# The down product of a decoder layer as seven products of halves, with sums of activations made in gate and up

## The chip, the cores and the metric

The kernel runs on one core of one Trainium2 chip. The metric is the device time of one execution in microseconds (us); less is better. Three runs of the kernel before gave 2863.46, 2863.54 and 2865.74, median 2863.54 us. TensorE is the matmul engine, VectorE (DVE), ScalarE (ACT) and GpSimd (POOL) are the elementwise engines, and SyncE (SP) issues most of the DMAs.

## What is computed

One inference step of a decoder layer over 2048 prompt tokens and 8 sample tokens, all in float32. The part that matters here is its last:

```
def swiglu(h, w_gate, w_up, w_down):
    return (jax.nn.silu(h @ w_gate) * (h @ w_up)) @ w_down

xp = xp + mix_out(y_conv, y_fox, y_mem, out_norm_g[l], w_out[l])
xp = xp + swiglu(rmsnorm(xp, norm2_g[l]), w_gate[l], w_up[l], w_down[l])
y_prompt = rmsnorm(xp, final_norm_g)
```

The width D is 1024 and D_FF is 2816, so `w_gate` and `w_up` are 1024 x 2816 and `w_down` is 2816 x 1024. The projections, the attention and the output product come ahead of it.

## The kernel before

The program runs in stages with a barrier of all engines between them: `project_all`, `attend`, `combine`, `gate_up`, `down`. Each float32 product is three matmuls on split operands: a high part (`_hi`, made by ScalarE) and a rest (`_lo`, made by VectorE or GpSimd): hi x hi, hi x lo, lo x hi.

**gate_up** (from about 1440 to 2340 us). The tokens are cut into three slices of 2 x 344, 2 x 344 and 2 x 340 (`WIDTHS`, `STARTS`); in a slice the two halves a11/a21 and a12/a22 are the two halves of the tokens against two blocks of 128 rows of D_FF. An item is one product of 256 columns of `w_gate` (even g) or `w_up` (odd g) with a slice. 22 items make a slice, 66 the stage. Each item is done by seven products of halves (`ORDER`: b11, t2, t3, t1, b21, t4, b22), 12 matmuls each. The weights of an item (1 MB) come by `weights(g)` on SP into `raw[g % 2]`; GpSimd makes four combinations t1 to t4 (`combos`, L2312 to L2317) and the rest of two base blocks (`base_lo`, L2325); ScalarE makes the high parts (`base_hi` L2357 and L2358, `combos_hi` L2348), VectorE the rests (`combos_lo` L2414, L2424). VectorE adds up the seven products: u2 (L2459), u3 (L2465), u4 (L2474), and the four quarters (L2436). For a gate item the quarters go to `silu`; for an up item each is multiplied at once with its `silu` (L2440), and after the fourth `s.act` is raised. SP waits for that and stores the quarters into `act_turned`, two DMAs of 128 x 2 x 344, and in the last slice two small ones with the 8 sample tokens (L2297).

What sets the order on SP: in iteration g it first issues the weights of item g + 2, then, if g is an up item, waits for `s.act` and issues the stores. So the weights of the gate item g + 3 are issued right behind the stores of the up item g. GpSimd takes up the combinations of g + 2 after those of g + 1 were split (`t_lo`), since there is one buffer for them; ScalarE splits them after its copy of b11 (L2387).

**down** (2341 to 2859 us). The product is done in two halves of 512 columns, each over 16 tiles of 128 tokens: 32 groups (n) of 22 x 3 matmuls of 128 x 512 (L2836 to L2838). The 22 weight blocks of a half stay on chip; the first 8, and the activations of tile 0, are loaded ahead, in gate_up. A tile of activations is 1.4 MB in rows of 512 B. Residual rows come from DRAM (`x1`), the half sum goes back to `x1` and is read again for the second half, where the final norm follows (ScalarE square, GpSimd root, VectorE scaling).

## Time and profile before

| | us |
|---|---|
| median of three runs | 2863.54 |
| span of the profiled execution | 2858.8 |
| gate_up, about | 900 |
| down, first to last matmul | 506.7 (2343.7 to 2850.4) |

| engine | busy us | share |
|---|---|---|
| TensorE | 2690.6 | 94% |
| VectorE | 1712.7 | 60% |
| GpSimd | 1610.4 | 56% |
| ScalarE | 1172.5 | 41% |

The profile is one execution, and its times count from the start of its span. Busy shares are means over stages. A row of a timeline has the start, the duration, the engine, the line and what was written from what was read; a bracket at its end says how long the engine stood idle ahead of it, and what ended that.

### The profile page before, as it was taken

How to read it: one execution, taken by the hardware profiler on the slowest of the kernel's cores; microseconds unless marked ns; L12 is line 12 of the kernel's file. 1: busy time of each engine (PE TensorE's matmuls, PEld its weight loads, DVE VectorE, ACT ScalarE, POOL GpSimd, SP SyncE). 2: the span in 40 equal slices, each digit the busy share in tenths (PEclk: the TensorE clock that was granted, in tenths of full speed). 3: DMA queues.
4: the chain of work that ended last, by engine and by line, in shares of the span. 5: the costliest groups of instructions: out<-in, count | busy, mean ns of one | idle time of the engine just before them, and what ended most of it. 6: DMA issues, size and time to landing. Idle time of an engine off the chain costs nothing. (4 is left out here: it accounts for less than half of the span.)

```text
span 2858.8 us, 42028 instructions
## 1 busy us (share of the span) xinstructions
PE 2690.6 (94%) x15009; PEld 2420.4 (85%) x15009; DVE 1712.7 (60%) x2248; ACT 1172.5 (41%) x1961; POOL 1610.4 (56%) x907
## 2 busy tenths in 40 slices
PE   8999999888888988899989999999999999999998
PEld 7998989777777767677789999999999987888887
DVE  5365686587777877676475657555756563224332
ACT  4212312477677777633343334333433332113222
POOL 3476688488798888465566665666655630000111
PEclk9999999899999999999989999999999999999999
DMA  6587889655565566675533323433255447445553
GB/s 211 172 269 249 269 269 306 159 143 163 154 174 153 163 172 178 202 245 194 186 110 119 115 89 121 126 102 119 79 119 144 103 110 213 127 135 162 166 161 110
DMA packets 451021, 468.87 MB, mean 164 GB/s; under 512 B 121959, under 2 KB 347042, under 8 KB 449782
## 3 DMA queue, kind: packets, MB, share of 16 engines
q1 hardware_dynamic: 431662, 443.82, 52.7%
q10 hardware_dynamic: 18864, 21.32, 2.1%
q8 instruction: 120, 1.97, 0.3%
q0 software_dynamic: 288, 1.05, 0.1%
q14 instruction: 87, 0.71, 0.1%
HBM read 384.96 MB, written 81.14 MB: 163 GB/s over the span
## 5 line engine op out<-in xcount | busy, mean ns | idle before, releaser
L2514 PE MATMUL ps_gate_up<-h_hi,w_hi 128*128 128x344 f32 (+1 forms) x1848 | 593.3, 321 | 27.3 <-DVE h_lo L2429 10.1
L2516 PE MATMUL ps_gate_up<-h_hi,w_lo 128*128 128x344 f32 (+1 forms) x1848 | 593.4, 321 | 0.0
L2515 PE MATMUL ps_gate_up<-h_lo,w_hi 128*128 128x344 f32 (+1 forms) x1848 | 592.9, 321 | 0.0
L2514 PEld LDWEIGHTS ps_gate_up<-h_hi,w_hi 128*128 128x128 f32 x1848 | 349.5, 189 | 31.2 <-issue 12.0
L2515 PEld LDWEIGHTS ps_gate_up<-h_lo,w_hi 128*128 128x128 f32 x1848 | 349.8, 189 | 0.0
L2516 PEld LDWEIGHTS ps_gate_up<-h_hi,w_lo 128*128 128x128 f32 x1848 | 349.7, 189 | 0.0
L878 PE MATMUL ps_proj<-w_hi,h_hi 128*128 128x428 f32 (+1 forms) x800 | 288.6, 361 | 9.7 <-ACT proj_out L602 9.6
L879 PE MATMUL ps_proj<-w_lo,h_hi 128*128 128x428 f32 (+1 forms) x800 | 285.0, 356 | 0.0
L880 PE MATMUL ps_proj<-w_hi,h_lo 128*128 128x428 f32 (+1 forms) x800 | 284.3, 355 | 0.0
L2836 PE MATMUL ps_down<-wd_hi,act_hi 128*128 128x512 f32 x704 | 275.7, 392 | 5.9 <-DVE wd_lo L2745 5.9
L1583 DVE TENSOR_TENSOR p_lo<-ps_turned,p_hi 128x512 fp32r<-128x512 f32 (+1 forms) x352 | 214.4, 615 | 106.0 <-ACT p_hi L1475 104.3
L2837 PE MATMUL ps_down<-wd_lo,act_hi 128*128 128x512 f32 x704 | 274.9, 390 | 0.0
L2838 PE MATMUL ps_down<-wd_hi,act_lo 128*128 128x512 f32 x704 | 274.9, 390 | 0.0
L2654 POOL TENSOR_SCALAR rstd<-sum_squares 128x1 f32<-128x1 f32 x15 | 12.1, 807 | 462.3 <-ACT stock L2693 462.3
L2312 POOL TENSOR_TENSOR stock<-common 128x512 f32<-128x512 f32 x65 | 95.1, 1462 | 275.3 <-DMA common<-in_w_gate 178.6
L1475 ACT ACTIVATE p_hi<-ps_turned 128x512 fp32r<-128x512 f32 (+1 forms) x352 | 187.2, 540 | 139.3 <-PE ps_turned L1406 138.2
L1406 PE MATMUL ps_turned<-ident,probs 128*128 128x128 f32 x1216 | 195.6, 277 | 46.7 <-ACT probs L1456 18.3
L1406 PEld LDWEIGHTS ps_turned<-ident,probs 128*128 128x128 f32 x1216 | 147.8, 142 | 97.5 <-ACT probs L1456 25.1
L2414 DVE TENSOR_TENSOR w_lo<-stock,w_hi 128x2048 fp32r<-128x2048 f32 x66 | 170.2, 2579 | 62.0 <-ACT w_hi L2348 61.9
L2760 DVE TENSOR_TENSOR common<-ps_down,common 128x512 f32<-128x512 f32 x32 | 22.1, 691 | 296.7 <-PE ps_down L2838 296.7
L2325 POOL TENSOR_TENSOR w_lo<-common,w_hi 128x1024 fp32r<-128x1024 f32 x65 | 162.7, 2504 | 52.8 <-ACT w_hi L2358 52.8
L1333 POOL TENSOR_TENSOR common<-common,scores 128x2048 f32<-128x2048 f32 x43 | 157.9, 3673 | 53.4 <-DMA common<-in_cache_v 53.4
(337 smaller groups left out, 6337.8 us busy)
## 6 DMA issues: line engine op xcount, KB each, us to landing
stock<-in_cache_k SPq DMA_DIRECT2D x192, 256.0 KB, 3.4
common<-in_cache_v SPq DMA_DIRECT2D x172, 256.0 KB, 3.0
common<-in_w_gate SPq DMA_DIRECT2D x33, 1024.0 KB, 6.4
common<-in_w_up SPq DMA_DIRECT2D x33, 1024.0 KB, 6.0
stock<-act_turned SPq DMA_DIRECT2D x16, 1408.0 KB, 8.0
act_raw<-act_turned SPq DMA_DIRECT2D x16, 1408.0 KB, 7.9
page_v<-in_cache_v SPq DMA_DIRECT2D x84, 256.0 KB, 3.1
common<-in_w_in SPq DMA_DIRECT2D x44, 428.0 KB, 4.8
```

Source lines behind the costliest of these rows:

```text
L878: pe.matmul(ps[:, bank, 0:w], a_hi, w_hi[:, d, :], start=(j == 0 and d == 0), stop=False)
L879: pe.matmul(ps[:, bank, 0:w], a_hi, w_lo[:, d, :], start=False, stop=False)
L880: mm = pe.matmul(ps[:, bank, 0:w], a_lo, w_hi[:, d, :], start=False, stop=(j == 3 and d == 1))
L1406: turned = pe.transpose(out[:, r * P:(r + 1) * P], probs(u.head, QCH * u.ch + r, u.j * P, (u.j + 1) * P), c.ident[:])
L1475: act.activation(a.p_hi[:, m % PARTS, r0 * P:], ps_t[:, bank_of["unit", m], r0 * P:], ACT.Copy).then_inc(s.t_hi, 1)
L1583: dve.tensor_tensor(a.p_lo[:, m % PARTS, r0 * P:], ps_t[:, bank_of["unit", m], r0 * P:], a.p_hi[:, m % PARTS, r0 * P:].bitcast(F32), ALU.s ...
L2514: pe.matmul(acc, a_hi, h_hi[:, m, d, 0:n], start=d == 0, stop=False)
L2515: pe.matmul(acc, a_hi, h_lo[:, m, d, 0:n], start=False, stop=False)
L2516: mm = pe.matmul(acc, a_lo, h_hi[:, m, d, 0:n], start=False, stop=d == H - 1)
L2836: pe.matmul(acc, a_hi[:, n % 2, f, :], w_hi[:, f, :], start=first, stop=False)
L2837: pe.matmul(acc, a_hi[:, n % 2, f, :], w_lo[:, f, :], start=False, stop=False)
L2838: mm = pe.matmul(acc, a_lo[:, n % 2, f, :], w_hi[:, f, :], start=False, stop=end)
```

## The change

**In down.** Tokens are paired: half of the tokens (1024, in 8 tiles) against the other half, even blocks of 128 rows of `w_down` against odd ones, left 512 columns against right 512. The four-by-four block product is done as seven products of halves, a pass over 8 tiles for each (`PASSES`: m2, m4, m5, m3, m1, m6, m7), 11 blocks x 3 matmuls a tile: 56 groups of 33. Five of the passes need a sum or difference of two weight blocks, made by GpSimd from a staged pair (`combine_weight`), all but m2 and m5. The residual rows (8 MB) are loaded once into `acc` on chip; each pass adds its product there in one or two places (`ADDED`), and the final norm runs in the last two passes. Nothing goes back to `x1`. The sample's 88 matmuls stay.

**In gate and up.** For each up item VectorE also makes the three sums and two differences of quarters that down needs (`act_sums`). All seven go to `act_combined`, which is laid out for down: [pass, tile, partition, block, token]. An item's columns are cut where a tile of 128 tokens ends (`run_pieces`): three pieces in the first and last slice, four in the middle one, once for the sums and once for the quarters and differences. Sums are written over `silu`, so the gate item's b21 quarter waits for the sum stores (`sum_stored`). The sample tokens are split 4 and 4 over the two halves (`PROMPT`, `turned_columns`), and one store of 16 B rows takes the place of two of 32 B rows.

The core of the diff (of `gate_up` and `down`):

```diff
+                        for p, at, t, n in run_pieces(g // ITEMS):
+                            dst = scratch.act_c[0:3, p, :, j, at:at + n].rearrange("m p t -> p m t")
+                            sp.dma_start(dst, sums_of(g)[:, :, t:t + n]).then_inc(s.sum_stored if g < N - 1 else c.last_act, 16)
+                        for p, at, t, n in run_pieces(g // ITEMS):
+                            dst = scratch.act_c[3:7, p, :, j, at:at + n].rearrange("m p t -> p m t")
+                            sp.dma_start(dst, out_of(g)[:, :, t:t + n]).then_inc(s.stored if g < N - 1 else c.last_act, 16)
...
+                def act_sums(g, which):
...
+                    if which == 0:
+                        dve.tensor_tensor(one, a11, a22, ALU.add)
+                    elif which == 1:
+                        dve.tensor_tensor(two, a21, a22, ALU.add).then_inc(s.summed, 1)
+                        dve.wait_ge(s.summed, 2 * q + 1)
+                        dve.tensor_tensor(a21[:, 0:kept], a21[:, 0:kept], a11[:, 0:kept], ALU.subtract)
+                    else:
+                        dve.tensor_tensor(five, a11, a12, ALU.add).then_inc(s.summed, 1)
+                        dve.wait_ge(s.summed, 2 * q + 2)
+                        dve.tensor_tensor(a12[:, 0:kept], a12[:, 0:kept], a22[:, 0:kept], ALU.subtract).then_inc(s.act, 1)
...
-                    e, t = divmod(n, NT)
-                    if n >= 4:
-                        pe.wait_ge(s.res, n - 3)
-                    for f in range(FT):
+                    m, p = divmod(n, TILES)
+                    if n >= BANKS:
+                        pe.wait_ge(s.res, n - BANKS + 1)
+                    for j in range(J):
...
+                    for a, e, op in ADDED[PASSES[m]]:
+                        to = acc[:, a, p, e * BLK:(e + 1) * BLK]
+                        done = dve.tensor_tensor(to, to, ps[:, n % BANKS, :], op)
+                    done.then_inc(s.res, 1)
...
+                act_tile(1)
+                residual_rows(1, 0)
+                weight(PILE)
+                sp.wait_ge(c.last_act_s, 16)
+                sp.dma_start(samp_raw[:, :, 0:2], scratch.act_s).then_inc(s.s_in, 16)
+                for p in range(1, TILES):
+                    residual_rows(1, p)
```

VectorE in an up item of gate_up, before: u3, then quarter and product four times with u4 between (`u_105` and `u_106` are the buffers of u2 and u3, `stock` holds the copy of b11).

```order
L2465 TENSOR_TENSOR u_106<-u_105,ps_gate_up 128x344
L2436 TENSOR_TENSOR act<-u_106,ps_gate_up 128x344
L2440 TENSOR_TENSOR act<-act,silu 128x344
L2474 TENSOR_TENSOR u_105<-u_105,ps_gate_up 128x344
L2436 TENSOR_TENSOR act<-stock,ps_gate_up 128x344
L2440 TENSOR_TENSOR act<-act,silu 128x344
L2436 TENSOR_TENSOR act<-u_106,ps_gate_up 128x344
L2440 TENSOR_TENSOR act<-act,silu 128x344
L2436 TENSOR_TENSOR act<-u_105,ps_gate_up 128x344
L2440 TENSOR_TENSOR act<-act,silu 128x344
```

The same place now, from the second quarter (b21) on.

```order
L2486 TENSOR_TENSOR act<-stock,ps_gate_up 128x344
L2490 TENSOR_TENSOR act<-act,silu 128x344
L2499 TENSOR_TENSOR silu<-act 128x344
L2486 TENSOR_TENSOR act<-u_106,ps_gate_up 128x344
L2490 TENSOR_TENSOR act<-act,silu 128x344
L2501 TENSOR_TENSOR silu<-act 128x344
L2503 TENSOR_TENSOR act<-act 128x344
L2486 TENSOR_TENSOR act<-u_105,ps_gate_up 128x344
L2490 TENSOR_TENSOR act<-act,silu 128x344
L2505 TENSOR_TENSOR silu<-act 128x344
L2507 TENSOR_TENSOR act<-act 128x344
```

Five operations whose operands all lie in SBUF have come between the quarters and behind the last of them, ahead of `s.act`.

SP in the middle slice of gate_up, before: the stores of an up item, the next gate weights, the next up weights, and again.

```order
L2295 DMA act_turned<-act 128x688 x2
L2267 DMA common<-in_w_gate 128x8x256
L2267 DMA common<-in_w_up 128x8x256
L2295 DMA act_turned<-act 128x688 x2
L2267 DMA common<-in_w_gate 128x8x256
```

The same place now.

```order
L2340 DMA act_combined<-silu 128x3x40
L2340 DMA act_combined<-silu 128x3x128 x2
L2340 DMA act_combined<-silu 128x3x48
L2343 DMA act_combined<-act 128x4x40
L2343 DMA act_combined<-act 128x4x128 x2
L2343 DMA act_combined<-act 128x4x48
L2312 DMA common<-in_w_gate 128x8x256
L2312 DMA common<-in_w_up 128x8x256
```

Eight stores stand where two stood, between `s.act` and the load of the gate weights.

## Rows read from the trace of the kernel before

**Rows 1.** The page: the span, and busy time of each engine.
```profile
span 2858.8 us, 42028 instructions
...
PE 2690.6 (94%) x15009; PEld 2420.4 (85%) x15009; DVE 1712.7 (60%) x2248; ACT 1172.5 (41%) x1961; POOL 1610.4 (56%) x907
```

**Rows 2.** Stretches: us, busy PE, PEld, DVE, ACT, POOL (count), clock, DMA share, GB/s.
```profile
1600.00:2340.00 740.00, 723.26 (x4575) 720.11 (x4573) 460.26 (x618) 270.95 (x335) 455.26 (x272) 1.00 0.38 109
...
2400.00:2500.00 100.00, 100.00 (x443) 82.84 (x442) 26.54 (x21) 18.56 (x14) 0.00 (x0) 1.00 0.47 126
```

**Rows 3.** Timeline of a pair of items in the last slice, by engine.
```profile
2127.68 0.37 SPq L2295 DMA_DIRECT2D act_turned<-act  x1
...
2129.69 0.40 SPq L2267 DMA_DIRECT2D common<-in_w_gate  x1
...
2137.85 1.29 POOL L2312 TENSOR_TENSOR stock<-common 128x512 f32<-128x512 f32 x1 [7.93 <-DMA common<-in_w_gate]
...
2148.05 0.49 DVE L2465 TENSOR_TENSOR u<-u,ps_gate_up 128x340 f32<-128x340 f32 x1
...
2154.25 0.37 SPq L2295 DMA_DIRECT2D act_turned<-act  x1
```

**Rows 4.** ScalarE's copies of b11 there, and TensorE's waits from 2080 to 2344.
```profile
2125.42 0.45 ACT L2387 ACTIVATE stock<-ps_gate_up 128x340 f32<-128x340 f32 x1 [0.23 <-PE ps_gate_up L2516]
...
2151.54 0.46 ACT L2387 ACTIVATE stock<-ps_gate_up 128x340 f32<-128x340 f32 x1 [0.23 <-PE ps_gate_up L2516]
...
PE ps_gate_up L2514 <- DVE w_lo L2424: 4.2, 5, 1.3
```

**Rows 5.** Timeline: GpSimd and a product of VectorE beside each other.
```profile
2150.76 1.57 POOL L2315 TENSOR_TENSOR stock<-common,stock 128x512 f32<-128x512 f32 x1
...
2153.82 2.69 POOL L2325 TENSOR_TENSOR w_lo<-common,w_hi 128x1024 fp32r<-128x1024 f32 x1
...
2151.63 1.07 DVE L2440 TENSOR_TENSOR act<-act,silu 128x340 f32<-128x340 f32 x1
```

**Rows 6.** Timeline in the middle slice: stores of two pairs, GpSimd's start.
```profile
1826.81 0.81 SPq L2295 DMA_DIRECT2D act_turned<-act  x2
...
1853.33 0.81 SPq L2295 DMA_DIRECT2D act_turned<-act  x2
...
1861.15 1.30 POOL L2312 TENSOR_TENSOR stock<-common 128x512 f32<-128x512 f32 x1 [4.86 <-DMA common<-in_w_gate]
```

**Rows 7.** DMA issues of the whole run: count, KB each, median us to landing.
```profile
act_turned<-act SPq DMA_DIRECT2D x44, 344.0 KB, 3.1
...
h_turned<-h_turned SPq DMA_DIRECT2D x16, 512.0 KB, 4.4
...
fox<-o_out SPq DMA_DIRECT2D x32, 128.0 KB, 2.0
...
act_sample<-act SPq DMA_DIRECT2D x20, 4.0 KB, 6.0
```

**Rows 8.** Down: one matmul line (first, last start), the accumulation's group, a tile's split.
```profile
L2836 PE MATMUL ps_down<-wd_hi,act_hi x704: 389/389/794, 2343.7 to 2850.4; 128*128 128x512 f32 x176
...
L2760 DVE TENSOR_TENSOR common<-ps_down,common 128x512 f32<-128x512 f32 x32 | 22.1, 691 | 296.7 <-PE ps_down L2838 296.7
...
2366.87 3.16 DVE L2750 TENSOR_TENSOR act_lo<-act_raw,act_hi 128x1408 fp32r<-128x1408 f32 x2 [0.58 <-ACT act_hi L2677]
```

**Rows 9.** From gate_up to down: timeline, TensorE's longest wait, the clock.
```profile
2338.45 0.51 DVE L2440 TENSOR_TENSOR stock<-stock,silu 128x340 f32<-128x340 f32 x1
...
2341.10 0.84 ACT L2677 ACTIVATE act_hi<-stock 128x768 fp32r<-128x768 f32 x1 [13.99 <-PEq L84]
...
PE ps_down L2836 <- DVE wd_lo L2745: 5.9, 1, 5.9
...
2345.00:2350.00 5.00, 5.00 (x13) 3.42 (x13) 5.00 (x8) 4.82 (x10) 0.00 (x0) 0.54 0.76 234
```

**Rows 10.** TensorE's longest wait at the turn to the middle slice.
```profile
1746.04 0.65 PE L2514 MATMUL ps_gate_up<-h_hi,w_hi 128*128 128x344 f32 x1 [3.53 <-DVE h_lo L2429]
```

More of the change, by code:

```diff
@@ L2212, in gate_up @@
         names = ("w_in0 w_in1 t_step t_made t_hi t_lo b_hi b_lo d_lo a11_in h_in s_step h_hi h_lo b_first done p1 u2 u3 u4 c22 c11 c21 c12 silu "
-                 "act stored s_stored ahead")
+                 "quarter summed act stored sum_stored s_stored ahead")
         with stage(nc, names) as (block, s):
@@ L2223, in out_of, with sums_of, stored_before, all_but_sample @@
             def out_of(g):
-                return last_out if g == N - 1 else act_out
+                return last_out[:, 0:4] if g == N - 1 else act_out
+            def sums_of(g):
+                return last_out[:, 4:7] if g == N - 1 else sil[:, 0:3]
+            def stored_before(q):
+                return 16 * sum(len(run_pieces(k // PAIRS)) for k in range(q))
+            def all_but_sample(g):
+                return PROMPT[g // ITEMS]
             def done(g, name):
@@ L2636, in _ @@
                 sp.wait_ge(s.s_normed, 1)
                 sp.dma_start(io.y_sample, xs[0:DB, :]).then_inc(s.s_stored, 16)
-                for slot in range(3):
-                    sp.wait_ge(stored[slot], 16 * ((N - slot + 2) // 3))
+                for t in range(2 * TILES - 3, 2 * TILES):
+                    store(t)
+                sp.wait_ge(s.stored, 16 * sum(len(segments(*tile_of(t))) for t in range(2 * TILES)))
                 sp.wait_ge(s.s_stored, 16)
@@ L2701, in left_normalise @@
-                def left_normalise():
-                    n = N - 1
-                    act.wait_ge(s.rstd, NT)
-                    act.wait_ge(s.left_gained, 1)
-                    act.activation(x[:, n % 3, 0:BLK], x[:, n % 3, 0:BLK], ACT.Copy, scale=rstd[:, NT - 1:NT]).then_inc(s.left_normed, 1)
-                    act.wait_ge(s.left_normed, 1)
-                    act.dma_start(io.y_prompt[SEQ - P:SEQ, 0:BLK], x[:, n % 3, 0:BLK]).then_inc(s.left_stored, 16)
-                for j in range(FT):
+                    cols = LEFT if t == 2 * TILES - 1 else slice(0, D)
@@ L2836, in _ @@
-                        pe.matmul(acc, a_hi[:, n % 2, f, :], w_hi[:, f, :], start=first, stop=False)
-                        pe.matmul(acc, a_hi[:, n % 2, f, :], w_lo[:, f, :], start=False, stop=False)
-                        mm = pe.matmul(acc, a_lo[:, n % 2, f, :], w_hi[:, f, :], start=False, stop=end)
-                        if n == NT - 1 and not end:
-                            mm.then_inc(s.w_used, 1)
-                    mm.then_inc(s.made, 1)
-                    if t == 0:
-                        for f in range(FT - BEHIND, FT):
-                            sample_products(e, f)
@@ L2845, in _ @@
-                    if t == 1:
+                        if p == 0:
+                            pe.wait_ge(s.w_lo, m * J + j + 1)
+                        out = ps[:, n % BANKS, :]
+                        pe.matmul(out, a_hi[:, n % 2, j, :], w_hi[:, slot, :], start=first, stop=False)
+                        pe.matmul(out, a_hi[:, n % 2, j, :], w_lo[:, slot, :], start=False, stop=False)
+                        mm = pe.matmul(out, a_lo[:, n % 2, j, :], w_hi[:, slot, :], start=False, stop=end)
```

509 lines of the change are left out of this document (298 added, 211 removed).

## Prediction

> **What bounds the kernel now.** The page comes first: TensorE is busy for 94% of the span [rows 1], so only a place where TensorE has little left to hide counts. The stretches come next: down runs at 443 matmuls in 100 us, 225.7 ns each, without a gap; gate and up look relaxed, with VectorE and GpSimd busy for 460 and 455 of 740 us [rows 2]. Those shares suggest that extra VectorE work in gate and up is free. The timeline of one pair of items (a gate item, an up item) in the last of the three token slices says something else, and it decides my forecast.
>
> From one pair to the next there runs a closed chain: VectorE finishes the up item's quarters; SP issues the activation stores, and only behind them the load of the gate weights three items on; GpSimd makes their four combinations; ScalarE and VectorE split these; VectorE then takes up the next up item's quarters. Its legs [rows 3]: first store to weight issue 2.01 us (2127.68 to 2129.69), issue to GpSimd's start 8.16, to VectorE's u3 10.20 (2137.85 to 2148.05), through the quarters to the next first store 6.20. The sum is 26.57 us. TensorE needs 26.12 us for the pair (copies of b11 at 2125.42 and 2151.54), so the chain is already the slower one there, and TensorE waits five times for w_lo, 4.2 us together [rows 4]. In the middle slice the stores come 26.52 us apart, which is TensorE's pace; its chain is the first leg, 7.82 us from store to GpSimd [rows 6], plus 10.20 and 6.20 as above: 24.2. So 2.3 us a pair are spare there, and none in the last slice. I use the middle slice for the first one too.
>
> **What the change does, step by step.**
>
> *Down, matmuls.* 32 groups of 22 x 3 become 56 groups of 11 x 3: 1848 for 2112. The rows give 704 for one of the three lines [rows 8]; the 88 matmuls of the sample stay 88. 264 x 0.2257 = **-59.6 us**, all on TensorE, which has no gap there.
>
> *Down, start.* From ScalarE's first piece at 2341.10 to the last matmul at 2850.4 are 509.3 us, against 2202 x 0.2257 = 497.0 of matmuls: 12.3 us lost to a late start, to 5.9 us of waiting for wd_lo and to the clock: 0.54 on average from 2345 to 2350, so 0.5, its 1.2 GHz level, until about 2349.6 [rows 8, 9]. After: the first piece is 3 wide instead of 6, so TensorE starts about 1.7 us in and loses some 2.9 us (half of 2343.7 to 2349.6) to the low clock, 4.6 together; one tile needs 11 weight blocks with 10 loaded ahead. The barrier comes later by two VectorE adds (1.1) behind the last product at 2338.45 and by four more stores on SP at 0.42 (1.7): 2.8. Net 4.6 + 2.8 - 12.3 = **-4.9 us**. What may be late here is the load of tile 2, which SP issues behind 3.5 MB of residual rows: with it 5.9 MB are in the queue, 19 us at 234 GB/s / 0.76 = 308 GB/s [rows 9] and 2 us to split, against a need at 4.6 + 14.9 = 19.5 us. That is 0 to 2 us late, which I put into the next item.
>
> *Down, rest.* Per tile of 33 x 0.2257 = 7.45 us VectorE has one or two accumulations of 0.69, a split of half the width that takes 3.16 us now [rows 8], and now and then weights at 0.6 each. Its heaviest tile, the last of a pass, has 2 x 0.69 + 1.6 + 8 x 0.6 = 7.8 us, which the bank depth of five and the weights' lead cover. Six changes of pass at 0 to 1.3 us: 0 to 8, I take **+3**. The tail (add, square, root, scale, store) keeps its length.
>
> *Gate and up, VectorE.* Each up item gets five SBUF-only operations, three sums and two differences, inside the last leg, before `s.act`, as the order of VectorE in the part on the change shows. Here the rows show something that a mean hides. A product that started at 2151.63 took 1.07 us and ended at 2152.70; GpSimd's combination ran from 2150.76 to 2152.33. It ended 0.37 us after the GpSimd operation that ran when it came, and the add ahead of it, from PSUM, took its usual 0.5 [rows 5]. The quarters fall into GpSimd's four combinations and its base_lo (2153.82, 2.69 us), since both start from the same t_lo. Walking the new order through these times: the first sum waits for 2152.33 and ends at 2152.70; the t4 add to 2153.2; its product waits for the fourth combination, to 2154.2; the second sum waits for base_lo's end at 2156.51, to 2156.9; then a difference, an add, a product, a sum and a difference at 0.52, to 2159.5. Before it was 2154.25: **+5.2 us** a pair. Bounds: five times 0.5 = 2.5 if nothing is blocked, five times 1.57 = 7.8 if each meets a combination. I take the walk.
>
> The Trainium skill, "SBUF — State Buffer", section "Who interferes with whom", says that a VectorE instruction with two SBUF inputs and a GpSimd instruction that reads SBUF exclude each other for a whole instruction. The rows agree for the products. By the rule the new sums and differences, which no row of before shows, stand under the same lock, and the leg grows by 5.2 us; were they free of it, by 2.5, which is a rival below.
>
> *Gate and up, stores.* Behind `s.act` SP now issues six stores (eight in the middle slice) instead of two, and the gate weights queue behind all of them. Bytes go from 4 to 7 quarters, and in pieces of at most 512 B: 7 x 3 x 128 = 2688 (3584 in the middle slice) where 512 of 1376 B stood. The lower bound is SP's issue alone, +4 x 0.42 = 1.7 us (+2.5). The upper one goes by h_turned, 1024 pieces of 512 B landing in 4.4 us, against 256 pieces of act_turned in 3.1 [rows 7]: 1.7 ns a piece, +3.7 us (+5.2). I take **+3.0** and **+4.0**, since part of the flow lies beside the issue. In the last slice one sample store replaces two of 32 B rows, which land in 6.0 us [rows 7]; they are why its first two legs are 10.17 and not 7.82, so this can move -2.4 to +2.4: I take 0.
>
> *The sum of the chain.* The first slice: 5.2 + 3.0 - 2.3 spare = 5.9 us on 9 pairs, 53. The middle one: 5.2 + 4.0 - 2.3 = 6.9 on 10, 69. The last: 5.2 + 3.0 = 8.2 on 10, 82. Together **+204 us**. At the two turns between slices VectorE is the bound already (TensorE waits 3.53 us for h_lo at 1746.04 [rows 10]), and five more operations stand before h_lo: **+5**. Waits of this size drop the clock to its lower level after each, as behind the gap in rows 9; TensorE then has several spare microseconds in the pair, so this costs nothing more while the chain is the longer one.
>
> All: 2858.8 - 59.6 - 4.9 + 3 + 204 + 5 = 3006.3 us of span; the median of the runs is 4.7 us above the profiled span: **3011**.
>
> **Rivals.**
>
> *The adds and stores are hidden.* By the busy shares it would be so, and the new waits on the stores (`stored`, `sum_stored`) come most of an item after them. Then only down and the turns count: 2858.8 - 61.5 + 5 + 4.7 = **2807**, faster. It decides if the chain keeps below 26.5 us, and against it stands that in the last slice the chain is over TensorE's pace by the rows, with 0.45 us a pair. Chance 0.12.
>
> *No blocking, and only issue time counts.* VectorE +2.5, stores +1.7 (+2.5; +1.1 in the last slice): 1.9 x 9 + 2.7 x 10 + 3.6 x 10 = 80 us, **2887**. It is the lower end of both bounds at once. Chance 0.15.
>
> *Short pieces are slow.* Of the pieces 896 an up item (1792 in the middle slice) are shorter than 512 B. If each cost what the sample's 256 did (2.35 us / 256 = 9.2 ns, 7.5 above the others), that is 6.7 us more a pair (13.4), 261 us in all: **3270**; half of it gives 3140. Against it: fox's stores of 256 B pieces, 512 of them, land in 2.0 us [rows 7]. Chance 0.17.
> The Trainium skill, "DMA: Bandwidth & Descriptors", section "Specifications", has transfers below 512 B done by read-modify-write; no row splits their price from their number.
>
> **How the numbers follow.** Forecast 0.56 (2 us a pair either way on 29 pairs: 2953 to 3069), hidden 0.12, unblocked 0.15, slow pieces 0.17. The range 2875 to 3150 leaves out the hidden case and the upper part of the slow one. A measurement of this kernel can tell 0.2% (5.7 us) from no change. Faster by more than that 0.13, within it 0.02, slower 0.85.
>
> **What would show it.** Right: gate stores of successive pairs 32 to 35 us apart, TensorE waiting for w_lo some 30 times, 5 to 8 us each, clock below 1 in gate and up; the new adds ending 0.37 us after GpSimd operations; first store to GpSimd's start at 11 to 12 us; down, from its first matmul, in some 442 us. Wrong: pairs still 26.5 us apart (hidden), or 28 to 30 (unblocked), or first store to GpSimd above 15 us, most in the middle slice (slow pieces); down above 455 us would mean that its loads or the changes of pass bind.

## The result, and the profile after

The changed kernel takes **3009.5 us** (median of four runs, 3003.0 to 3013.1) against 2863.5 before: a ratio of 1.051, 95% interval 1.0496 to 1.0527. The forecast was 3011. The sum came out right; several of its terms did not, as the experiments show.

The page: span, and busy time of each engine (after).

```profile
span 3011.4 us, 42326 instructions
...
PE 2700.8 (90%) x14745; PEld 2431.9 (81%) x14745; DVE 1964.5 (65%) x2560; ACT 1187.9 (39%) x2044; POOL 1696.9 (56%) x963
```

TensorE has 264 matmuls less and yet more busy time than in [rows 1]: part of it ran at the lower clock. The waits of TensorE (after; engine, line, what for: us in total, times, longest):

```profile
PE ps_gate_up L2587 <- DVE w_lo L2474: 124.7, 32, 7.4
PE ps_gate_up L2587 <- DVE h_lo L2479: 23.8, 7, 5.6
...
PE ps_gate_up L2587 <- DVE w_lo L2472: 14.2, 1, 14.2
...
PE ps_down L2972 <- DVE wd_lo L2880: 8.6, 1, 8.6
...
PE ps_down L2972 <- DVE act_lo L2885: 5.8, 1, 5.8
```

32 waits for w_lo stand where there were eight before (five of those eight in the last slice [rows 4]). The pair of items that answers to [rows 3], in the last slice (timeline; start, us, engine):

```profile
2258.91 1.47 SPq L2340 DMA_DIRECT2D act_combined<-silu  x3
2260.42 1.71 SPq L2343 DMA_DIRECT2D act_combined<-act  x3
...
2262.83 0.76 SPq L2312 DMA_DIRECT2D common<-in_w_gate  x1
...
2270.48 1.29 POOL L2362 TENSOR_TENSOR stock<-common 128x512 f32<-128x512 f32 x1 [14.56 <-DMA common<-in_w_gate]
...
2280.61 0.50 DVE L2530 TENSOR_TENSOR u<-u,ps_gate_up 128x340 f32<-128x340 f32 x1
...
2291.99 1.46 SPq L2340 DMA_DIRECT2D act_combined<-silu  x3
```

The same closed chain, now 33.08 us a turn: first store to weight issue 3.92 (2.01 before), issue to GpSimd 7.65 (8.16), GpSimd to u3 10.13 (10.20), u3 to the next store 11.38 (6.20). TensorE still needs 26.1, and waits for the rest. In that last leg VectorE meets GpSimd's base_lo as [rows 5] had it for a product:

```profile
2286.31 2.68 POOL L2375 TENSOR_TENSOR w_lo<-common,w_hi 128x1024 fp32r<-128x1024 f32 x1
...
2286.76 2.61 DVE L2501 TENSOR_TENSOR silu<-act 128x340 f32<-128x340 f32 x1
```

The second sum, 0.5 us of work, takes 2.61: it ends at 2289.37, 0.38 us after GpSimd's operation (2288.99). The clock there (after; stretch: us, busy PE, PEld, DVE, ACT, POOL, clock, DMA share, GB/s):

```profile
2110.00:2300.00 190.00, 162.43 (x945) 159.79 (x945) 131.51 (x164) 60.14 (x73) 93.00 (x55) 0.89 0.35 97
```

Where the 152.6 us of span (3011.4 against 2858.8) came from, by TensorE's first and last matmuls of each stage (the last of all three lines):

| | before | after | difference |
|---|---|---|---|
| up to gate_up's first matmul | 1436.6 | 1444.6 | +8.0 |
| gate_up, first to last | 900.9 | 1097.9 | +197.0 |
| between the two | 6.2 | 8.9 | +2.7 |
| down, first to last | 507.2 | 452.6 | -54.6 |
| behind the last | 7.9 | 7.4 | -0.5 |

The legs of the chain as means over the pairs of a slice, from the timelines of SP, GpSimd and VectorE (first slice 8 pairs, the others 10; the turns between slices left out). The leg from the first store to GpSimd's start is split at the issue of the gate weights.

| us | to issue | to GpSimd | to u3 | to store | pair |
|---|---|---|---|---|---|
| before: first, middle, last | 0.9, 0.9, 2.1 | 6.4, 6.8, 8.2 | 12.7, 12.0, 10.2 | 6.5, 6.5, 6.2 | 26.5, 26.1, 26.7 |
| after | 3.3, 4.3, 4.0 | 6.6, 6.1, 7.7 | 11.3, 11.0, 10.1 | 11.4, 11.5, 11.4 | 32.6, 32.9, 33.2 |

In the first two slices before, the leg to u3 holds the spare time (it waits for TensorE there); its bare length is 10.2, or 13.3 in the six pairs with a token sum, of which e9 and e10 tell.

### The profile page after: what moved, and what is told of

The parts are those of the page before. It is cut to its first block and busy times, and to the rows that moved or that the text cites. A ratio compares the mean times of both kernels' runs of the same rounds, so it can differ in the third digit from the quotient of the medians.

```text
span 3011.4 us, 42326 instructions
## 1 busy us (share of the span) xinstructions
PE 2700.8 (90%) x14745; PEld 2431.9 (81%) x14745; DVE 1964.5 (65%) x2560; ACT 1187.9 (39%) x2044; POOL 1696.9 (56%) x963
## 3 DMA queue, kind: packets, MB, share of 16 engines
q0 software_dynamic: 288, 1.05, 0.1%
## 5 line engine op out<-in xcount | busy, mean ns | idle before, releaser
L2587 PE MATMUL ps_gate_up<-h_hi,w_hi 128*128 128x344 f32 (+1 forms) x1848 | 623.6, 337 | 165.2 <-DVE w_lo L2474 124.7
L2588 PE MATMUL ps_gate_up<-h_lo,w_hi 128*128 128x344 f32 (+1 forms) x1848 | 617.3, 334 | 0.0
L2589 PE MATMUL ps_gate_up<-h_hi,w_lo 128*128 128x344 f32 (+1 forms) x1848 | 616.5, 334 | 0.0
L2362 POOL TENSOR_TENSOR stock<-common 128x512 f32<-128x512 f32 x65 | 94.6, 1455 | 508.0 <-DMA common<-in_w_gate 424.8
L2588 PEld LDWEIGHTS ps_gate_up<-h_lo,w_hi 128*128 128x128 f32 x1848 | 372.1, 201 | 0.0
L878 PE MATMUL ps_proj<-w_hi,h_hi 128*128 128x428 f32 (+1 forms) x800 | 289.5, 362 | 10.4 <-ACT proj_out L602 10.3
L2972 PE MATMUL ps_down<-wd_hi,act_hi 128*128 128x512 f32 x616 | 242.3, 393 | 14.4 <-DVE wd_lo L2880 8.6
L2973 PE MATMUL ps_down<-wd_lo,act_hi 128*128 128x512 f32 x616 | 241.6, 392 | 0.0
L2974 PE MATMUL ps_down<-wd_hi,act_lo 128*128 128x512 f32 x616 | 241.4, 392 | 0.0
L2770 POOL TENSOR_TENSOR stock<-common 128x512 f32<-128x512 f32 x55 | 87.3, 1598 | 271.3 <-DMA common<-in_w_down 270.9
L2818 ACT ACTIVATE act_hi<-stock 128x768 fp32r<-128x768 f32 (+2 forms) x114 | 83.1, 774 | 314.4 <-PE ps_down L2974 282.8
L2896 DVE TENSOR_TENSOR acc<-acc,ps_down 128x512 f32<-128x512 f32 x96 | 62.4, 685 | 194.5 <-PE ps_down L2974 194.5
```

Of the source, the lines that this page charges most:

```text
L878: pe.matmul(ps[:, bank, 0:w], a_hi, w_hi[:, d, :], start=(j == 0 and d == 0), stop=False)
L2587: pe.matmul(acc, a_hi, h_hi[:, m, d, 0:n], start=d == 0, stop=False)
L2588: pe.matmul(acc, a_hi, h_lo[:, m, d, 0:n], start=False, stop=False)
L2589: mm = pe.matmul(acc, a_lo, h_hi[:, m, d, 0:n], start=False, stop=d == H - 1)
L2972: pe.matmul(out, a_hi[:, n % 2, j, :], w_hi[:, slot, :], start=first, stop=False)
L2973: pe.matmul(out, a_hi[:, n % 2, j, :], w_lo[:, slot, :], start=False, stop=False)
```

## The experiments

Gate_up and down are counted from their first to their last matmul in each run's trace.

| run | time us | ratio to before | gate_up | down |
|---|---|---|---|---|
| the changed kernel | 3009.5 | 1.051 | 1097.9 | 452.6 |
| e1 weights ahead of the stores | 2811.6 | 0.9826 (0.9795 to 0.9857) | 903.4 | 451.8 |
| e2 without the sums' operations | 2842.6 | 0.9942 (0.9922 to 0.9961) | 931.7 | 452.7 |
| e3 long rows, two stores | 2983.6 | 1.0439 (1.0408 to 1.0470) | 1065.5 | 455.8 |
| e4 before, five operations from SBUF | 2994.5 | 1.0455 (1.0427 to 1.0482) | 1036.8 | 510.3 |
| e5 before, five with a PSUM operand | 2943.0 | 1.0283 (1.0253 to 1.0313) | 982.1 | 507.9 |
| e6 tile 2 early, turned stores at 32 B | 3001.3 | 1.0492 (1.0460 to 1.0523) | 1093.3 | 452.1 |
| e7 e1, 32 B, residual rows spread | 2803.7 | 0.9799 (0.9772 to 0.9826) | 904.4 | 444.3 |
| e8 before, weights ahead of the stores | 2857.2 | 0.9993 (0.9980 to 1.0007) | 895.5 | 508.9 |
| e9 token sums one item later | 3007.7 | 1.0500 (1.0483 to 1.0518) | 1098.4 | 452.6 |
| e10 token sums in GpSimd's idle time | 2989.8 | 1.0441 (1.0421 to 1.0462) | 1078.8 | 452.5 |
| e11 before, no sample stores | 2857.5 | 0.9993 (0.9980 to 1.0005) | 899.2 | 506.8 |
| e12 stores 16 B off | 3190.6 | 1.1160 (1.1128 to 1.1192) | 1276.7 | 460.3 |

**e1: is it a closed chain?** SP's order, and nothing else:

```diff
+                weights(2)
                 for g in range(N):
-                    weights(g + 2)
+                    if is_up(g):
+                        weights(g + 2)
+                        weights(g + 3)
...
                     if is_up(g):
                         sp.wait_ge(s.act, g // 2 + 1)
```

> The changed kernel with SP's order altered: the gate weights three items on are issued ahead of the up item's activation stores, not behind them. The VectorE operations and the stores are the same. My theory (a closed chain through VectorE's quarters, SP's stores, the gate weights and GpSimd): the weights no longer wait for VectorE's last leg or the stores, the chain is open, pairs come at TensorE's 26.2 us or a little over in place of 33, and the time is 3009.5 - 29 x 6.5 = 2820 us, 2805 to 2850. Rival 1 (VectorE's blocked operations fill the pair by themselves, whatever the weights do): only the store leg goes, 3 to 4 us a pair, 2895 to 2920 us. Rival 2 (the stores' short pieces load the DMA engines and slow the weights behind or beside them): weights still land late, above 2930 us.

2811.6 us: 198 less, and the first theory's figure was 2820. In the last slice (timelines, and a stretch as above):

```profile
2233.03 0.37 SPq L2312 DMA_DIRECT2D common<-in_w_gate  x1
2243.90 1.46 SPq L2343 DMA_DIRECT2D act_combined<-silu  x3
...
2246.63 1.61 POOL L2365 TENSOR_TENSOR stock<-common 128x512 f32<-128x512 f32 x1 [4.22 <-DVE w_lo L2467]
...
2240.59 2.19 DVE L2493 TENSOR_TENSOR act<-act,silu 128x340 f32<-128x340 f32 x1
...
2110.00:2300.00 190.00, 190.00 (x1224) 190.00 (x1223) 148.07 (x198) 67.58 (x85) 117.91 (x72) 1.00 0.52 145
```

The weights are issued 10.9 us ahead of the stores, and GpSimd waits for its one buffer (the split, w_lo), not for the load. VectorE's operations are still held up by GpSimd (a product of 0.5 us takes 2.19), and its leg from u3 (2232.88) to the stores is 11.02 us, yet TensorE has not one idle moment from 2110 to 2300, at full clock. So 194.5 of gate_up's 197.0 us were the chain's (1097.9 to 903.4), and its parts are free once it is open. The rivals (VectorE's work fills the pair; the stores slow the weights anyway) fall.

**e8: how much of that is the order's own?** The same edit in the kernel before.

> The kernel before with only SP's order altered: gate weights ahead of the up item's stores. It tells how much of the 1.7% by which the changed kernel with this order beats the kernel before is the order's own. Theory (the chain is over TensorE's pace only in the last slice, by 0.45 us a pair): 4 to 8 us less, some 2856 us, so that nearly all of the gain is down's. Rival (the chain cost the kernel before more than its waits show): 15 us less or more.

Gate_up is 5.4 us shorter (900.9 to 895.5), TensorE's waits for w_lo fall from 7.3 us in eight to 1.6 in three, and the pairs of the last slice come 26.1 us apart, for 26.7; the time is 2857.2, a ratio of 0.9993 whose interval holds 1. So the chain cost the kernel before next to nothing, and the 1.7% of e1 are down's.

**e2: the price of VectorE's five operations.** The calls of `act_sums` are taken out, and `s.act` is raised by the last product.

> The changed kernel without the five VectorE operations for each up item (the three sums and two differences are left out; what is stored in their place is whatever the buffers hold). Stores and their sizes stay. Theory (these operations stand under the exclusion with GpSimd and cost 5.2 us of the chain): a pair goes from 33 to 28 us, 29 x 5.2 + 5 for the turns = 156 us less, 2854 us, 2840 to 2870. Rival (each costs only its own 0.5 us): 29 x 2.5 + 2 = 75 us less, 2935 us.

Gate_up 1097.9 to 931.7, 166 us for 156 expected; a pair of the last slice takes 27.9 us, as I had said, and its last leg 6.2. One wait row of TensorE (in the changed kernel 124.7, 32, 7.4):

```profile
PE ps_gate_up L2583 <- DVE w_lo L2474: 22.2, 16, 2.7
```

The operations cost 5.2 us a pair, twice their own time. What is left over the kernel before is 31 us. The stores are all that this run still adds to the chain; some of the 31 shows in the six pairs with a token sum (28.6 to 29.5 us each, for 26.6 to 27.3 before; e9 and e10 below), which had nothing to spare.

**e4 and e5: is it the exclusion with GpSimd?** Five more operations in the kernel before, at the places of the sums and differences, once on two SBUF tiles and once with the product in PSUM as one operand:

```diff
+                def five_more(g, which):
+                    n, q = width(g), g // 2
+                    dve.wait_ge(s.quarter, 4 * q + {0: 2, 1: 3, 2: 4}[which])
+                    one, two = out_of(g)[:, which, 0:n], out_of(g)[:, 3, 0:n]
...
+                    one, two = out_of(g)[:, which, 0:n], product(g, {0: "b21", 1: "t4", 2: "b22"}[which])
```

> The kernel before with five more VectorE operations for each up item, in the places of the three sums and two differences: each reads two SBUF tiles and writes a spare one (its result is used by nobody). No store is added or cut, nothing else moves. Theory (with SBUF operands alone they wait for the end of the GpSimd operation that runs when they come, as the sums do in the changed kernel): the VectorE leg grows by 5.2 us, of which 2.3 are spare in the first two slices: 2.9 x 19 + 5.2 x 10 + 3 for the turns = 110 us more than before, 2970 us, 2950 to 2985. Rival (VectorE's own time counts, 5 x 0.5): 0.2 x 19 + 2.5 x 10 = 29 us more, 2890 us.

> The same five operations at the same places of the kernel before, but one of the two operands of each is the product in PSUM, as the quarters' adds have it. Theory (such an operation doesn't wait for GpSimd and takes 0.5 us): the VectorE leg grows by some 2.5 us and the time by 30 us, to 2890 us, 2870 to 2910. Rival (what costs is more VectorE work between GpSimd's operations, whatever it reads): as long as with SBUF operands, near 2970 us.

e4 took 2994.5, e5 2943.0: 52 us apart, both slower than I had said. The legs from u3 to the store tell why: 6.2 before, 11.15 in e4 (+4.95), 9.5 in e5 (+3.3, not 2.5). First e4, then e5, in the last slice (timelines; L2317 is GpSimd's fourth combination, L2325 its base_lo):

```profile
2266.24 2.67 POOL L2325 TENSOR_TENSOR w_lo<-common,w_hi 128x1024 fp32r<-128x1024 f32 x1
...
2266.68 2.60 DVE L2447 TENSOR_TENSOR silu<-act 128x340 f32<-128x340 f32 x1
```

```profile
2243.65 1.45 POOL L2317 TENSOR_TENSOR stock<-common,stock 128x512 f32<-128x512 f32 x1
2245.05 2.41 POOL L2325 TENSOR_TENSOR w_lo<-common,w_hi 128x1024 fp32r<-128x1024 f32 x1
...
2244.40 0.50 DVE L2455 TENSOR_TENSOR silu<-act,ps_gate_up 128x340 f32<-128x340 f32 x1
...
2245.36 2.48 DVE L2444 TENSOR_TENSOR act<-act,silu 128x340 f32<-128x340 f32 x1
```

In e4 the added sum waits for base_lo's end. In e5 the added operations take their 0.5 us while GpSimd's fourth combination runs, as adds from PSUM do; but they push the last product, whose operands are both in SBUF, from in front of base_lo to behind its start, and it takes 2.48 us. So the exclusion is shown, and so is something that my rival of 2.5 us did not have: an operation that is not held up itself can still cost more than its length. The Trainium skill, "SBUF — State Buffer", section "Who interferes with whom", has a VectorE instruction with at most one SBUF input free of GpSimd, and one with two SBUF inputs in contention with GpSimd's reads; both rows agree.

The miss is 26 us in e4 (136 us of gate_up for 110) and 51 in e5 (81 for 30). With the legs as measured, +4.95 and +3.3, the sums would be 103 and 52. What is left, 33 and 29 us, lies in the first two slices. Some 17 us are the token sums of six pairs (e9 and e10 below), which my 2.3 us of spare time left out. Another 11 to 13 are a longer wait for the gate weights: from their issue to GpSimd's start 7.2 and 7.3 us in e4 and 7.0 and 7.3 in e5, for 6.4 and 6.8 before, with the same loads and stores; why is open.

**e3: the number of stores and pieces.** The scratch becomes [combination, partition, block, token]; an up item has two stores, of 3 and 4 times 1344 to 1376 B a partition.

```diff
-                        for p, at, t, n in run_pieces(g // ITEMS):
-                            dst = scratch.act_c[0:3, p, :, j, at:at + n].rearrange("m p t -> p m t")
+                        at, n = BASES[g // ITEMS], all_but_sample(g)
+                        for kept, source, landed in ((slice(0, 3), sums_of(g), s.sum_stored), (slice(3, 7), out_of(g), s.stored)):
+                            dst = scratch.act_c[kept, :, j, at:at + n].rearrange("m p t -> p m t")
```

> The changed kernel with the scratch of activations laid out as (combination, partition, pair, token) and not cut by tiles of 128 tokens: two stores an up item in place of six or eight, with pieces of 1344 to 1376 B, 896 in place of 2688 or 3584; the bytes are the same, and the down product loads its tiles in pieces of 512 B, 1408 a tile, in place of 5632 B. Theory (four or six more issues at 0.42 us and 1.7 ns for each further piece, part of it beside the issue): 2.5 to 4 us a pair less, 3009.5 - 29 x 3 = 2922 us, 2890 to 2950. Rival 1 (only the issues count): 1.7 x 19 + 2.5 x 10 = 57 us less, 2952 us. Rival 2 (bytes alone count, not pieces or issues): within 10 us of 3009. Down, from first to last matmul, keeps its 452 us; if the loads of short pieces bind there, it grows by 10 or more.

2983.6: 26 us less, a third of what I gave it, and less than even the rival by issues alone. (Gate_up is 32 us shorter in the trace, which is of the shortest of its four runs.) The last slice:

```profile
2264.26 0.37 SPq L2341 DMA_DIRECT2D act_combined<-silu  x1
...
2266.23 1.31 SPq L2312 DMA_DIRECT2D common<-in_w_gate  x1
...
2274.73 1.30 POOL L2360 TENSOR_TENSOR stock<-common 128x512 f32<-128x512 f32 x1 [13.46 <-DMA common<-in_w_gate]
```

The issue comes 1.95 us earlier (1.97 after the first store, not 3.92), but the load lands later behind it (8.50, not 7.65): the leg falls by 1.1 only. In the first two slices 2.2 and 3.3 us of issues go and 1.5 and 2.3 come back. While SP issues the stores their bytes already move, and the weights queue behind 1.2 MB (7 x 128 x 344 x 4 B) whether this is cut small or not. The kernel before has two stores in rows of the same length as e3, but 0.7 MB: from first store to GpSimd's start it takes 7.3 and 7.7 us in the first two slices, e3 9.2 and 9.3, the changed kernel 9.9 and 10.4. So of a store term of 2.6 and 2.7 us, 1.9 and 1.7 are bytes. Down is 3 us longer with tiles in pieces of 512 B (4.7 us to land, not 4.2).

**e9 and e10: a leg of 13.1 us.** In the changed kernel the leg to u3 is 10.2 us in most pairs, but 13.1 in six, three each in the first and the middle slice. There GpSimd makes a token sum (`s_combo`: a sum or difference of two parts of the next slice's tokens) between the combinations and base_lo (after; timeline):

```profile
1599.85 3.16 POOL L2289 TENSOR_TENSOR stock<-stock 128x1376 f32<-128x1376 f32 x1
1602.95 4.39 POOL L2375 TENSOR_TENSOR w_lo<-common,w_hi 128x1024 fp32r<-128x1024 f32 x1
...
1601.88 3.27 DVE L2464 TENSOR_TENSOR w_lo<-stock,w_hi 128x2048 fp32r<-128x2048 f32 x1 [4.72 <-ACT w_hi L2398]
```

Here the exclusion works both ways. VectorE's split of the combinations, which begins while the token sum runs, takes 3.27 us and not 2.3 to 2.5; and base_lo, which GpSimd takes up behind the token sum, takes 4.39 and not 2.4 to 2.7. In all six pairs base_lo ends 2.2 us after VectorE's split (here 1607.34, after 1605.15), as if it began only then.

e9 moves the three sums by one item (`i in (8, 12, 16)` to `(9, 13, 17)`):

> The changed kernel with the three token sums that GpSimd makes for the next slice (128 x 1376, 3.16 us each) moved by one item: behind the combinations of an up item's weights, where GpSimd then waits 14 us for the next load, not behind those of a gate item's, where they stand in the chain. Theory (in the traces of the changed kernel the leg from GpSimd's start to VectorE's u3 is 10.2 us in most pairs and 13.1 in the six or seven pairs with such a sum, a term that my sum did not have; before, it lay in the spare time): all pairs show 10.2 us, and gate and up lose 6 x 2.9 = 17 us: 1097.9 to some 1081 us from first to last matmul, 2992 us in all. Rival (the 13.1 us have another cause, such as the load of the next slice's tokens): no change, 3009 us.

3007.7, no change. The leg to u3 is 10.2 in all pairs, and the leg from u3 to the store is 14.2 to 14.3 in the six (e9; timeline):

```profile
1607.42 3.43 POOL L2289 TENSOR_TENSOR stock<-stock 128x1376 f32<-128x1376 f32 x1
...
1607.87 3.36 DVE L2501 TENSOR_TENSOR silu<-act 128x344 f32<-128x344 f32 x1
```

GpSimd's operation ends at 1610.85, VectorE's at 1611.23. I had looked for a place where GpSimd was idle soon after, and put the sum beside VectorE's exposed leg. e10 puts it where neither has to wait:

```diff
                     base_lo(g + 1)
+                    sc, i = g // ITEMS + 1, g % ITEMS
+                    if sc < SC and i in (8, 12, 16):
+                        pool.wait_ge(s.t_lo, g + 2)
+                        s_combo(pool, sc, ("s1", "s2", "s3")[(i - 8) // 4])
                     combos(g + 2)
```

> The changed kernel with the same three token sums at a third place: ahead of a gate item's combinations and behind the wait for the last split of weights, so that they run while GpSimd waits for the gate weights and VectorE has finished the up item's quarters, sums and differences. With the sums one item later (the run before this one) the 2.9 us had only moved from the leg to u3 (13.1 to 10.2) to the leg through the quarters (11.4 to 14.3), since VectorE's sums then waited for them. Theory (they cost 2.9 us a pair wherever they meet the chain, and nothing beside it): neither leg is longer in any pair, six pairs are 2.9 us shorter, gate and up go from 1098 to some 1081 us, 2992 us in all. Rival (some other operation of VectorE or ScalarE on the chain is held up instead): the six pairs keep their 33.8 to 35.7 us, 3008 us.

2989.8 us; gate_up 1078.8, 19.1 less for 17 expected. All pairs have 10.2 and 11.4 to 11.5 in the two legs (but two, with 12.5 and 11.8 in the second: the first pair of the stage and the second of the middle slice). So six times 2.9 us of the change's cost were GpSimd's token sums. They stood at the same place before, and had used up the spare time of their pairs. The one of [rows 6], whose stores begin at 1853.33, is such a pair (before; timeline):

```profile
1866.28 3.13 POOL L2244 TENSOR_TENSOR stock<-stock 128x1360 f32<-128x1360 f32 x1
```

Its leg to u3 is 13.29.

**e6 and e7: the start of down, and the turned stores.** TensorE's wait at down's third tile (after: TensorE and ScalarE, SP, and two stretches):

```profile
2574.66 0.79 PE L2972 MATMUL ps_down<-wd_hi,act_hi 128*128 128x512 f32 x1 [5.80 <-DVE act_lo L2885]
...
2572.77 1.47 ACT L2818 ACTIVATE act_hi<-stock 128x768 fp32r<-128x768 f32 x2 [11.70 <-DMA stock<-act_combined]
...
2552.36 5.35 SPq L2723 DMA_DIRECT2D acc<-x  x9
2557.76 0.43 SPq L2719 DMA_DIRECT2D stock<-act_combined  x1
...
2550.00:2573.00 23.00, 17.41 (x66) 13.93 (x66) 11.88 (x22) 9.21 (x21) 3.67 (x3) 0.87 1.05 318
2575.00:2580.00 5.00, 5.00 (x13) 3.84 (x13) 4.53 (x5) 1.47 (x2) 4.05 (x3) 0.50 0.84 279
```

The tile's load stands behind nine loads of residual rows and comes 5.8 us late; behind the gap the clock is at 0.50, its 1.2 GHz level, for these 5 us, which costs about 2.5 more. e6 issues `act_tile(2)` ahead of the residual rows; its second edit shifts the turned activations (`h_turned`, the input of gate_up, which the stage ahead of it stores transposed) by 8 tokens, not 4 (`2 * SHARE`, `APART = 344`, `TOKENS + 16`).

> The changed kernel with two small things undone that I had not priced well. First, in the down stage the activations of tile 2 are issued ahead of the residual rows. Theory: TensorE's 5.8 us wait at the third tile and the second fall of the clock behind it go, 6 to 9 us less between the first and the last matmul of down (452.1 to 443 to 446). Rival: the residual rows or the weights are late in their place, and down keeps 452. Second, the turned activations of the combine stage are shifted by 8 tokens (32 B) in scratch where the change shifts them by 4 (16 B), with the same number of stores and pieces. Theory: the stores of the last tiles land in 7.6 us against 4.5 before because their pieces start 16 B off a 32 B step; with 32 B they land in 4.5 to 5 us, and the first matmul of gate and up comes 2 to 5 us earlier than 1444.65. Rival: the number of stores and the 16 B rows of the sample are the cause, and the landing stays at 7 to 8 us. Together 2995 to 3001 us; if neither holds, 3009.

Down keeps 452.1: the wait has only gone one tile on, where it is 4.0 us for TensorE (e6):

```profile
2570.99 1.47 ACT L2820 ACTIVATE act_hi<-stock 128x768 fp32r<-128x768 f32 x2 [15.85 <-DMA stock<-act_combined]
```

The rival was right for down. For the turned stores the theory was: the 512 KB stores at the stage's end, before, after and in e6 (DMA issues from 1415 to 1445; KB each, median us to landing):

```profile
h_turned<-h_turned SPq DMA_DIRECT2D x2, 512.0 KB, 4.1
```

```profile
h_turned<-h_turned SPq DMA_DIRECT2D x2, 512.0 KB, 8.1
```

```profile
h_turned<-h_turned SPq DMA_DIRECT2D x2, 512.0 KB, 4.2
```

Same bytes, same 1024 pieces of 512 B, the sample's 16 B rows beside them in the last two. TensorE's wait at gate_up's start is 14.2 us after (12.5 to 14.6 in the runs that keep the 16 B), 9.5 in e6, 9.8 in e7 and 7.6 before.

e7 takes e1, the 32 B shift, and spreads the residual rows over the tiles of the first pass:

```diff
-                for p in range(1, TILES):
+                for p in (1, 2):
                     residual_rows(1, p)
...
+                    if n + 3 < TILES:
+                        residual_rows(1, n + 3)
                     for i in loads_at(n):
                         weight(i)
-                    if 1 <= n <= TILES:
-                        sp.wait_ge(s.res, n)
-                        residual_rows(0, n - 1)
+                    if 3 <= n <= TILES + 2:
+                        sp.wait_ge(s.res, n - 2)
+                        residual_rows(0, n - 3)
```

> The changed kernel with three things at once, as a version that may beat both. The gate weights ahead of the activation stores (2811.6 us by itself). The turned activations shifted by 8 tokens (32 B) where the change has 4 (16 B). And in down the residual rows of tiles 3 to 7 are issued one a tile, not all ahead of the activations of tile 2 (those of the other half three tiles later than now). Theory (the bytes of the residual rows, 3.5 MB, are what makes the third or the fourth tile's activations late; moving one load ahead only moved the stall): no wait for act_lo over 1 us, no second fall of the clock, down from first to last matmul in 443 to 447 us in place of 452; with some 3 us from the turned stores 2800 us, 2794 to 2808. Rival (the order of weights or the buffers of two tiles bind): a wait of 4 to 6 us stays and the time is 2808 to 2812.

2803.7 us, **2.0% faster than the kernel before** (0.9772 to 0.9826) and 6.8% faster than the changed one. Down takes 444.3; ScalarE waits 3.3 to 5.7 us for the loads of three of the first tiles, and TensorE for none (e7):

```profile
2362.78 1.48 ACT L2824 ACTIVATE act_hi<-stock 128x768 fp32r<-128x768 f32 x2 [3.33 <-DMA stock<-act_combined]
...
2360.00:2380.00 20.00, 20.00 (x89) 16.52 (x88) 8.99 (x13) 4.42 (x6) 5.50 (x5) 1.00 1.02 354
```

**e11 and e12: pieces that begin 16 B off.** The turned stores raised a doubt on [rows 7]: why do the activation stores of the last slice land in 6.1 us before, and those of the others in 3.1? The row that those did not have (before; DMA issues of the whole run):

```profile
act_turned<-act SPq DMA_DIRECT2D x20, 340.0 KB, 6.1
```

The halves are 340 tokens there, so the second piece of each row begins 16 B off a multiple of 32. e11 leaves the sample's stores out; e12 moves the changed kernel's scratch by 4 tokens (`at += j * P + 4`, rows 8 tokens longer).

> The kernel before without the sample's stores in the last slice (one store of the same tensor at the first pair stands for all of them, so the sample's output of the feed-forward part is not computed). In its last slice the activation stores land in 6.1 us against 3.1, and from first store to GpSimd's start are 10.4 us against 7.6. I had put this down to the sample's rows of 32 B; but half of the pieces of 1360 B begin 16 B off there. Theory (the 16 B): the landing stays at 5 us or more, the leg falls by 1.1 us of issues to some 9.2, the chain goes below TensorE's pace, and the time falls by about 5 us to 2855 to 2860. Rival (the sample's rows): the landing falls to 3.1 us and the leg to 7.6; the time comes out alike, so the trace decides.

> The changed kernel with its scratch of activations moved by 4 tokens, so that every stored piece begins 16 B off a multiple of 32 B; rows are 8 tokens longer, number and size of pieces stay, and down reads from 16 B further on. Theory (what the turned activations showed: 512 KB in 1024 pieces of 512 B land in 7.2 to 8.2 us where they begin at 16 B, and in 4.1 to 4.2 us where they begin at 32 B): the stores of a pair take some 3 us longer and the gate weights behind them land that much later, 29 x 3 = 90 us more, 3100 us, 3060 to 3150. Rival (in the turned activations the rows of 16 B beside them were the cause): 3009 us as before. Down keeps its 452 us if only writes mind where a piece begins.

e11's activation stores (whole run; first those of the two other slices):

```profile
act_turned<-act SPq DMA_DIRECT2D x44, 344.0 KB, 2.8
...
act_turned<-act SPq DMA_DIRECT2D x20, 340.0 KB, 6.1
```

Without the sample's stores it is still 6.1: the place of the pieces is the cause, not the sample. (A row of 1360 B also ends 16 B off where it begins on 32 B, and in e12 every piece both begins and ends off; no run tells the two apart.) The leg falls from 10.3 to 10.0, so even the 1.0 us of issues comes back as landing (8.2 to 8.9), as in e3. e12, and then the changed kernel:

```profile
act_combined<-act SPq DMA_DIRECT2D x64, 256.0 KB, 9.3
act_combined<-silu SPq DMA_DIRECT2D x64, 192.0 KB, 3.7
```

```profile
act_combined<-act SPq DMA_DIRECT2D x64, 256.0 KB, 2.8
act_combined<-silu SPq DMA_DIRECT2D x64, 192.0 KB, 2.3
```

3190.6 us, 181 more, twice what I expected. GpSimd starts 12.1, 13.3 and 12.3 us after the issue of the gate weights in the three slices, for 6.6, 6.1 and 7.7. Down is 8 us longer too (460.3), although the loads of its tiles land in 4.3 us as before. Its start shows where (e12; two waits of TensorE, and a stretch):

```profile
PE ps_down L2974 <- DVE wd_lo L2882: 11.2, 2, 8.6
PE ps_down L2974 <- DVE act_lo L2887: 8.4, 1, 8.4
...
2720.00:2725.00 5.00, 2.93 (x7) 2.38 (x8) 4.29 (x9) 4.84 (x11) 1.19 (x2) 0.50 1.31 105
```

A second wait for wd_lo (2.6 us) has come, and the one for tile 2 is 8.4 us, for 5.8. At the stage's start the DMA engines are fully busy and move 105 GB/s, with the last activation stores still among their work (the last lands at 2729.8), and the first loads of down stand behind them. The waits are 5.2 of the 8 us, and the lower clock behind each fits the rest; that it is the stores and not the shifted reads is read from these rows, not tested.

## Why the prediction was right, point by point

- **What bounds.** Right. Busy shares would have said that VectorE had room (65%, even after), and the chain's legs said that it did not. e1 is the proof: the same work, the chain open, 198 us less.
- **VectorE's leg.** +5.2 by the walk, 5.20 measured (6.20 to 11.40), and in e2 5.2. The bounds 2.5 and 7.8 held; the lower one was not to be had even with five operations that are free of GpSimd themselves (e5: 3.3).
- **Stores.** Over-priced: 3.0, 4.0 and 3.0 us a pair against 2.6, 2.7 and 1.3 (first store to GpSimd: 7.3, 7.7 and 10.3 before, 9.9, 10.4 and 11.6 after). The step that failed is the sum of issue time and piece time: they overlap. In the last slice the changed layout also brought a gain that I had not seen: no piece begins 16 B off there any more. I had "why its first two legs are 10.17 and not 7.82" down to the sample's rows of 32 B, and e11 says no.
- **Spare time.** 2.3 us a pair, from a first leg of the middle slice (7.82 us, to 1861.15) and a leg to u3 of 10.20 from the last one. The step that failed is that the two were put together: the very pair of the 7.82 holds a token sum, its leg to u3 is 13.29, and it had nothing to spare. Six pairs are so, and in the changed kernel the chain was longer for them than I took it for: 6 x 2.9 = 17 us, which e10 gave back (19).
- **The sum of the chain.** From store to store: first slice 53 forecast, 56 measured; middle 69 and 68; last 82 and 65; turns 5 and 7; the first pair of the stage 0 and 5; the end of the stage 0 and -3.5. Together 209 and 197. Stores too dear and token sums left out have cancelled in the first two slices. That the total was within 2 us is partly luck. So is the 4.7 us that I added for the median over the profiled span: between the two profiled runs the span grew by 152.6 us, for 147.5 forecast, and between the medians the time grew by 146.0.
- **The clock** at 0.91 to 0.92 in the three slices of gate_up cost nothing more, as said: the pairs are as long as their legs. It does make the waits shorter than my 5 to 8 us: they are 124.7 / 32 = 3.9 in the mean. In the stretch from 2110 to 2300 (945 matmuls, 5.6 pairs) TensorE is idle for 27.6 us, 4.9 a pair, and busy for 162.4, where 945 at e1's pace of 1224 in 190 us need 146.7: an estimate of 2.8 us a pair for the lower clock.
- **Down.** From ScalarE's first piece to the last matmul 509.3 before; forecast 64 less, measured 55 (2549.53 to 3003.5). The matmuls are as said. The step that failed is "0 to 2 us late": tile 2 was 5.8 us late and the clock fell once more, 8 us in all. My 308 GB/s was right (318 from 2550 to 2573), but at that rate 7.3 MB had moved when tile 2 was there (2572.77), not 5.9. Loads issued behind it, of weights and of tile 3, moved beside it, and so did the end of the last stores. And the clock I had counted only once. The forecast "down in some 442" was right for e7, 444.
- **Turned stores.** Put at zero without a word, and this was the plainest miss: gate_up began 8.0 us later. 6.5 of these are TensorE's longer wait for w_lo (of which 4.6 go with the 32 B shift of e6). The other 1.5 lie ahead of that wait, where they tell nothing: TensorE comes to it at 1423.5 to 1434.8 us in the fourteen traces, changed or not. The diff's `turned_columns` was a change to a stage that ends in a barrier, and I had looked only at its count of stores.
- **Rivals.** Hidden: it needed the chain under 26.5. The price I gave for that case, 2807, is what e1 (2812) and e7 (2804) reached once the order on SP was changed. Unblocked: excluded by e4 and e5. Short pieces: excluded for pieces on 32 B by e3; the Trainium skill, "DMA: Bandwidth & Descriptors", section "Specifications", has a read-modify-write below 512 B, and no run here shows its price by itself; e3's 26 us bound what pieces of 160 to 512 B in place of 1344 to 1376 B cost here, the issues with them.

## What to carry to other kernels

Before adding work to an engine that is idle a third of the time, walk the loop of waits that it stands in, issue queues included; if a load is queued behind a store that waits for that work, put the load ahead first, since then the added work (and the stores) are free as long as the matmul engine stays the slowest, as here, where that was worth 198 us. Look for that chain in more than one turn of the loop, since work that comes every few turns can have used up the spare time. Walk added operations against the other engine's timeline, since what they push may cost more than they do. And print where each DMA piece begins: 16 B off in DRAM turned a 1.05 into a 1.12.

## What was not expected of the hardware

- Stores to DRAM whose pieces begin 16 B off a multiple of 32 B: 512 KB in pieces of 512 B 8.1 us against 4.1 (and 4.2 with 32 B), 256 KB 9.3 against 2.8, 340-token rows with every second piece off 6.1 against 3.1 (all from issue to landing, what stands ahead in the queue included). As a whole kernel: 3190.6 against 3009.5 us. Whether the begin or the end of a piece matters, or other offsets, or loads, was not run.
- Issue time of stores hides in part under the bytes of the stores ahead: 1.95 us of issues taken away, and the short pieces with them, gave 1.1 (e3); 1.0 us of issues taken away gave 0.3 (e11).
- An operation of VectorE with two SBUF operands waits for the end of the GpSimd operation that runs when it comes, also for one of 3.43 us, beside which it takes 3.36; in each of the five kernels shown (after, e1, e4, e5, e9) it ends 0.37 to 0.38 us after it.
- GpSimd is held by VectorE as well: base_lo took 4.39 us behind a token sum, and ended 2.2 us after VectorE's split of the combinations, in each of six pairs of the changed kernel; it takes 2.4 to 2.7 elsewhere. This is read from the trace; no run tests it by itself.
